# Hybrid trunk step on one core: the shift of the first modulation is carried through the input product as one more streamed column, and x is loaded by tiles

## What is computed

```python
def layer(x, c, pool_prefix, conv_prefix, pos0, norm1, ...):
    mod = jax.nn.silu(c) @ w_ada + b_ada
    sh1, sc1, g1, sh2, sc2, g2 = jnp.split(mod[:, None, :], 6, axis=-1)
    h = rmsnorm(x, norm1) * (1.0 + sc1) + sh1
    z = h @ w_in                       # 1024 x 2048
    u, gate_b, gate_c, val = jnp.split(z, ...)
    pool_out = pool_mixer(u, ...)      # trailing means, per-group map
    conv_out = gate_b * conv3(gate_c * val)
    x = x + g1 * (concat(pool_out, conv_out) @ w_out)
    h2 = rmsnorm(x, norm2) * (1.0 + sc2) + sh2
    x = x + g2 * moe(h2)               # top 4 of 32 experts
    return x, pool_state, conv_state
```

## Time and profile before

| | |
|---|---|
| median of 3 runs | 1287.76 us (1287.5, 1287.76, 1290.37) |
| span of the profiled execution | 1285.4 us |
| PE busy | 1250.7 us, 97% |
| input product starts | 37.93 us |
| feature 3 ends (fourth feature) | 67.51 us |
| feature 8 starts | 101.75 us |

### The profile page before, as it was taken

How to read it: one execution, slowest core, us unless ns; L and a number is a source line. 1 busy time by engine, 2 the same in 40 slices (tenths; PEclk the granted TensorE clock), 3 DMA queues, 4 the chain that set the end, 5 groups by cost and what they waited for, 6 DMA issues and landing times.

```text
span 1285.4 us, 32056 instructions
## 1 busy us (share of the span) xinstructions
PE 1250.7 (97%) x14081; PEld 639.7 (50%) x14081; DVE 522.6 (41%) x822; ACT 91.2 (7%) x170; POOL 248.7 (19%) x333
## 2 busy tenths in 40 slices
PE   4999999899999999999999999999999999999997
PEld 2787755534433444444444444444444444444454
DVE  1133314566333333333333334444444444443356
ACT  3210011210000000000000000000000000000002
POOL 4502300031222222111221111111111111122100
PEclk9999999899999999999999999999999999999998
DMA  9986861289999999999999999999999999999993
GB/s 349 265 334 231 303 255 81 105 366 428 421 425 425 425 426 426 420 424 421 425 423 421 422 425 424 425 427 425 419 423 427 426 423 424 428 427 423 423 424 154
DMA packets 62290, 487.45 MB, mean 379 GB/s; under 512 B 10387, under 2 KB 19203, under 8 KB 36913
## 3 DMA queue, kind: packets, MB, share of 16 engines
q1 hardware_dynamic: 47442, 455.92, 85.4%
q0 software_dynamic: 11632, 20.85, 4.6%
q10 hardware_dynamic: 3183, 10.21, 2.0%
HBM read 468.35 MB, written 25.88 MB: 384 GB/s over the span
## 4 chain that ended last, share of the span: by engine, by line
PE 95%; DVE 2%; ACT 1%; DMA 1%; issue 1%; SPq 0%; DVEq 0%; ACTq 0%
PE acc L2024 51%; PE acc L2049 24%; PE acc L964 9%; PE acc L1022 4%; PE acc L892 2%; PE acc L2133 1%; PE acc L2002 1%; DMA x_sb<-in_x_sample 1%; PE acc L910 1%; ACT junk L537 0%; PE acc L2149 0%; DVE picked L1684 0%; PE acc L994 0%; PE acc L1018 0%; PE acc L1034 0%
## 5 line engine op out<-in xcount | busy, mean ns | idle before, releaser
L2024 PE MATMUL acc<-raw,ht 128*32 128x512 f32 x2928 | 320.5, 592 | 0.0
L2024 PE MATMUL acc<-raw_b,ht 128*32 128x512 f32 x2928 | 320.5, 592 | 0.0
L1741 DVE TENSOR_TENSOR g_sb<-acc,bias_gu 128x768 f32<-128x768 f32 x32 | 30.6, 957 | 519.0 <-PE acc L2024 519.0
L1460 POOL DMA_INDIRECT rows<-h_rows,row_next x90 | 93.4, 1038 | 689.6 <-DVE row_next L1625 625.7
L2024 PEld LDWEIGHTS acc<-raw_b,ht 128*32 128x32 f32 x2928 | 111.0, 110 | 203.2 <-issue 203.2
L2024 PEld LDWEIGHTS acc<-raw,ht 128*32 128x32 f32 x2928 | 110.1, 110 | 190.6 <-issue 186.6
L2049 PE MATMUL acc<-raw_b,at 128*32 128x256 f32 x2976 | 166.9, 379 | 0.0
L2049 PE MATMUL acc<-raw,at 128*32 128x256 f32 x2976 | 166.9, 379 | 0.0
L2049 PEld LDWEIGHTS acc<-raw_b,at 128*32 128x32 f32 x2976 | 112.4, 110 | 61.4 <-issue 17.2
L2049 PEld LDWEIGHTS acc<-raw,at 128*32 128x32 f32 x2976 | 112.4, 110 | 48.2
L964 PE MATMUL acc<-h_t,raw 128*128 128x288 f32 (+1 forms) x512 | 118.8, 393 | 1.1 <-DVE h_t L732 1.1
(11 more groups left out here) (282 smaller groups left out, 677.1 us busy)
## 6 DMA issues: line engine op xcount, KB each, us to landing
raw<-in_w_down SPq DMA_DIRECT2D x33, 2048.0 KB, 15.7
raw<-in_w_gate SPq DMA_DIRECT2D x31, 2048.0 KB, 9.1
raw<-in_w_up SPq DMA_DIRECT2D x31, 2048.0 KB, 13.4
raw_b<-in_w_gate SPq DMA_DIRECT2D x31, 2048.0 KB, 10.1
raw_b<-in_w_up SPq DMA_DIRECT2D x31, 2048.0 KB
raw_b<-in_w_down SPq DMA_DIRECT2D x31, 2048.0 KB
raw<-in_w_ada SPq DMA_DIRECT2D x24, 1024.0 KB, 11.6
expert_rows<-zeros ACTq DMA_DIRECT2D x1, 8704.0 KB, 31.7
```

What stands on the lines that cost most here:

```text
L1460: pool.indirect_dma_start(rows[:, b, :], None, h2_quarter, bass.IndirectOffsetOnAxis(ap=idx[:, b:b + 1], axis=0), bounds_check=Q * NTOK - ...
L1741: dve.tensor_tensor(g_sb[:, :, :], gate_of(i, 0), plus(0), ALU.add).then_inc(g_read, 1)
L2024: mm = pe.matmul(gu_of(i)[b][q * TB:(q + 1) * TB, :].rearrange("p (m n) -> p m n", m=2), ht_of(i)[:, b, k, :], w[:, kk, :, q * CW:(q + 1) ...
```

## The change

The first modulation is split: only the scale is applied to `h_t` for the prompt. The shift vector is written as column 544 of `h_t` (`SHIFT_COL`), so that the second half of each feature streams 289 columns instead of 288, and the product of shift and w_in comes out beside the tokens. ACT copies that column to `z_shift` (`shift_of`), and everything that reads a feature of the prompt adds it: as the bias of the ACT copy, or as the scalar of a `scalar_tensor_tensor` on DVE. For the sample tokens scale and shift are still applied to `h_t` by DVE, the shift after the chunks of SH1. PE starts with the first halves of features 0, 1 and 2 as soon as the scale is in, then runs SH1, and half of feature 3's first half, the turning of the shift, the rest, and after that the four second halves. Features 2 and 3 need PSUM of their own for the first half (`z_early`) and are copied in two pieces. The order of chunks becomes SC1, in 0 and 1, SH1, in 2 and 3, G1, in 4 and 5, and from there on as before. x is loaded tile by tile and squared tile by tile, the tiles are turned into three PSUM tiles instead of one and earlier in the order, and the columns of scale and shift get PSUM and semaphores of their own. Two small memsets on POOL move ahead, so that ACT can start to square earlier. Some semaphores of the expert part are shared to make room (`tile_in`, `sum_step`); the waits there stay what they were.

```diff
@@
-        order = ada_chunks(SC1) + ada_chunks(SH1) + in_chunks(0, 4) + ada_chunks(G1) + in_chunks(4, 6)
+        order = ada_chunks(SC1) + in_chunks(0, 2) + ada_chunks(SH1) + in_chunks(2, 4) + ada_chunks(G1) + in_chunks(4, 6)
@@ sync
-            sp.dma_start(x_sb[:, 0:PT, :], x_prompt[0].rearrange("(t p) d -> p t d", p=P)).then_inc(x_loaded, 16)
-            sp.dma_start(x_sb[0:NS, PT, :], x_sample.rearrange("b t d -> (b t) d")).then_inc(x_loaded, 16)
+            for t in range(PT):
+                sp.dma_start(x_sb[:, t, :], x_prompt[0, t * P:(t + 1) * P, :]).then_inc(tile_in[t], 16)
+            sp.dma_start(x_sb[0:NS, PT, :], x_sample.rearrange("b t d -> (b t) d")).then_inc(tile_in[PT], 16)
@@ gpsimd
-            pool.wait_ge(h_mod_a, KT // 2)
+            pool.wait_ge(shift_col, 1)
@@ scalar
-            act.wait_ge(x_loaded, 32)
             act.wait_ge(consts, 2)
             for t in range(TT):
+                act.wait_ge(tile_in[t], 16)
                 square(t, 0)
...
+            for t in range(TT):
+                turned(f"n{t}", t, row_ps[t])
+            empty_cols(0)
...
             for k in range(KT // 2, KT):
                 act.activation(h_t[:, k, 0:SEQ], h_t[:, k, 0:SEQ], ACT.Identity,
-                               scale=cols[:, 0, k % 2, k // 2, 0:1],
-                               bias=cols[:, 1, k % 2, k // 2, 0:1]).then_inc(h_mod_a, 1)
+                               scale=cols[:, 0, k % 2, k // 2, 0:1]).then_inc(h_mod_a, 1)
+            empty_cols(1)
+            act.wait_ge(cols_free, 2)
+            act.activation(h_t[:, :, SHIFT_COL:SHIFT_COL + 1].rearrange("p (q h) o -> p h q o", h=KT // Q),
+                           cols[:, 1, :, :, 0:1], ACT.Copy).then_inc(shift_col, 1)
...
+            def shift_of(f):
+                act.wait_ge(z_done, f + 1)
+                act.activation(z_shift[:, f:f + 1], z_col[f % 2], ACT.Copy).then_inc(z_shift_ready, 1)
+
             def leave(f, dst, dst_s):
-                act.wait_ge(z_done, f + 1)
-                act.activation(dst.rearrange("p (b n) -> p b n", b=2), z_prompt[f % 2], ACT.Copy)\
-                    .then_inc(z_evac, 1)
+                shift_of(f)
+                act.wait_ge(z_shift_ready, f + 1)
+                halves = dst.rearrange("p (b n) -> p b n", b=2)
+                if f in z_early:
+                    for b in range(2):
+                        act.activation(halves[:, b, :], z_half(f, b)[:, 0:PH], ACT.Identity, bias=z_shift[:, f:f + 1])\
+                            .then_inc(z_evac, 1)
+                else:
+                    act.activation(halves, z_prompt[f % 2], ACT.Identity, bias=z_shift[:, f:f + 1]).then_inc(z_evac, 1)
                 act.activation(dst_s, z_sample[f % 2], ACT.Copy).then_inc(z_evac, 1)
@@ vector (features 8 to 11; 12 to 15 likewise)
-                dve.tensor_tensor(vext[...], z_prompt[f % 2], gate_c[...], ALU.mult)
+                dve.wait_ge(z_shift_ready, f + 1)
+                dve.scalar_tensor_tensor(out=vext[...], in0=z_prompt[f % 2], scalar=z_shift[:, f:f + 1],
+                                         in1=gate_c[...], op0=ALU.add, op1=ALU.mult)
@@ tensor
             ada_chunk(SC1, 0)
+            unit_transposes(0)
             ada_chunk(SC1, 1)
-            transposes("n0", 0, 0)
+            unit_transposes(1)
+            unit_transposes(2)
             ada_chunk(SC1, 2)
+            unit_transposes(3)
+            unit_transposes(4)
             ada_chunk(SC1, 3)
-            transposes("n1", 1, 0)
             pe.wait_ge(scale_ready, 1)
-            turn_cols("cols_sc", SC1)
...
+            turn_cols(SC1)
+            def half_product(f, b, k_first=0, k_end=KT):
+                w = chunk("in", f // 2)
+                lo_, hi_ = ((0, PH), (PH, SHIFT_COL + 1))[b]
+                for j in range(k_first, k_end):
+                    if f == 0 and b == 0:
+                        pe.wait_ge(*((h_mod_d, j + 1) if j < KT // 2 else (h_mod_a, j + 1 - KT // 2)))
+                    mm = pe.matmul(z_half(f, b), w[:, j, (f % 2) * P:(f % 2 + 1) * P], h_t[:, j, lo_:hi_],
+                                   start=(j == 0), stop=(j == KT - 1))
+                return mm
+            def early_chunks():
+                for f in range(3):
+                    half_product(f, 0)
+                ada(SH1)
+                half_product(3, 0, 0, KT // 2)
+                pe.wait_ge(ada_added, ADA_AT[SH1] + 1)
+                pe.wait_ge(cols_free, 1)
+                turn_cols(SH1)
+                half_product(3, 0, KT // 2, KT)
+                pe.wait_ge(h_mod_d, KT // 2 + KT // Q)
+                pe.wait_ge(shift_col, 1)
+                for f in range(4):
+                    if f >= 2:
+                        pe.wait_ge(z_evac, evacuated(f - 2))
+                    half_product(f, 1).then_inc(z_done, 1)
```

More of the change, by code:

```diff
@@ L128, in hybrid_step @@
         slot_loaded = [sem(f"slot_loaded{s}") for s in range(XSLOTS)]
+        tile_in = [sem(f"tile_in{t}") for t in range(TT)]
         part = ExitStack()
@@ L213, in hybrid_step, with z_half, evacuated @@
         z_sample = [z[:, 1, PH:PH + NS].rearrange("p (s t) -> p s t", t=DEC_T) for z in zt]
+        z_col = [z[:, 1, PH + NS:PH + NS + 1] for z in zt]
+        z_early = {2: acc_y[:, 1, 0:PH], 3: tp[:, 1, 0:PH]}
+        def z_half(f, b):
+            return z_early[f] if b == 0 and f in z_early else zt[f % 2][:, b, 0:PH if b == 0 else PH + NS + 1]
+        def evacuated(f):
+            return sum(3 if g in z_early else 2 for g in range(f + 1))
+        row_ps = [tp, acc_g, acc_u, tp, acc_g]
+        cols_ps = acc_y[:, 0, QW:2 * QW]
         pm_p = [tp[:, 0, :], tp[:, 1, :], acc_y[:, 1, :], tp[:, 0, :]]
@@ L607, in _ @@
                     empty_states()
+            for f in range(2 * GR, 4 * GR):
+                shift_of(f)
             for g in range(GR):
@@ L719, in unit_rows @@
                     .then_inc(h_ready, 1)
-            for t in range(3):
+            for t in range(TT):
                 unit_rows(t)
@@ L725, in _, with sample_half @@
             scale_rows(SC1, n1_rows)
[L726 to L730, removed]
+            dve.wait_ge(tp_free, TP["n4"] + 1)
+            dve.wait_ge(cols_free, 1)
             for k in range(KT // 2):
                 dve.tensor_scalar(h_t[:, k, 0:SEQ], h_t[:, k, 0:SEQ], cols[:, 0, k % 2, k // 2, 0:1],
[L733 to L739 removed]
+                                  None, ALU.mult).then_inc(h_mod_d, 1)
+            def sample_half(i, half):
+                v = h_t[:, :, SEQ:NTOK].rearrange("p (q h) (s t) -> p h q s t", q=Q, t=DEC_T)[:, half]
+                c = cols[:, i, half, :, 1:NC].unsqueeze(3).to_broadcast([P, Q, DEC_B, DEC_T])
+                return dve.tensor_tensor(v, v, c, (ALU.mult, ALU.add)[i])
+            for half in range(KT // Q):
+                step(sample_half(0, half))
+            add_ada(SH1)
+            dve.wait_ge(cols_free, 2)
+            for half in range(KT // Q):
+                sample_half(1, half).then_inc(h_mod_d, 1)
             def windows(src_, n, ext, buf):
@@ L810, in _ @@
                 v = conv[:, g, 0:SEQ].rearrange("p (b n) -> p b n", b=2)
-                dve.tensor_tensor(v, v, z_prompt[f % 2], ALU.mult).then_inc(conv_ready, 1)
+                dve.wait_ge(z_shift_ready, f + 1)
+                dve.scalar_tensor_tensor(out=v, in0=z_prompt[f % 2], scalar=z_shift[:, f:f + 1], in1=v,
+                                         op0=ALU.add, op1=ALU.mult).then_inc(conv_ready, 1)
                 v = by_seq(conv[:, g, SEQ:NTOK])
@@ L903, in take, with transposes @@
                     pe.wait_ge(tp_free, TP[name])
-            def transposes(name, t, base):
-                take(name)
+            def transposes(name, t, base, dst=tp, free=None):
+                if free is None:
+                    take(name)
+                else:
+                    pe.wait_ge(tp_free, free)
                 pe.wait_ge(h_ready, base + t + 1)
@@ L955, in project @@
                         pe.wait_ge(conv_s_ready, f - 3 * GR - 1)
[L956 to L969, removed]
+                    else:
+                        pe.wait_ge(z_evac, evacuated(f - 2))
+                    half_product(f, 0)
+                    half_product(f, 1).then_inc(z_done, 1)
+            early_chunks()
             pe.wait_ge(state_loaded, 16 * 4)
@@ L1212, in hybrid_step @@
             fn_loaded = sem("fn_loaded")
-            picked_in = [sem(f"picked_in{t}") for t in range(TT)]
             sum_step = sem("sum_step")
```

83 lines of the change are left out of this document (38 added, 45 removed).

## The result

The changed kernel takes 1292.1 us (median of 14 runs, 1290.03 to 1293.05) against 1288.29 us (1287.5 to 1290.37) for the kernel before: a ratio of 1.0026, with a 95% interval of 1.002 to 1.0033. It is slower by about 3.4 us. A second measurement gave 1.0031 (1.0021 to 1.0041). The prediction was 1290.0, with 1285 to 1298 and "same" as the likeliest. The loss is within the 0.3% that the prediction took as its line for "same", and yet clear of the noise.

A forecast was written before the change was run, and what follows sets the result against it. PE bounds the kernel (95% of the chain). Feature 3 -6.65 us, stand +6.2, clock +2.5, 289th column and small waits +0.2: +2.2 on 1285.4; the median stands 2.4 over that span: 1290.0 us, range 1285 to 1298.

The forecast's parts named there:

- "same": Whole kernel: time within 0.3% (3.9 us), with faster below 1283.9 and slower above 1291.6; chance 0.47.
- likeliest case: Whole kernel: early clock rise, PE stands before feature 8, clock falls; 1287.5 to 1292 us, chance 0.44.
- the early gain: Start through feature 3: product starts 10.5 us earlier, at 27.4; feature 3 ends 6.65 us earlier, at 60.85.
- the stand for chunk in 4: Before feature 8: PE waits 6.2 us, from 95.1 to 101.25, for that chunk to land.
- the half clock behind it: From feature 8: the pause lowers PE's clock, which returns after 3.4 to 5.6 us; price 2.5 us.
- rival 2: Start: tiles of x land together, squares start late, feature 3 ends some 4 us later; 1294 us, chance 0.08.
- The clock at the start: First chunks and tiles: unbroken work from 14.21, transposes included, raises PE's clock at 18.8, within 17.6 to 19.8.
- Rival 1: Start: transposes don't count, PE stays slow to the product at 32.5, nothing gained by feature 3; 1297.5 us, chance 0.26.
- The collision: Behind feature 3: five chunks (5.2 MB) start together with the zeros; chunk in 4 lands 40.4 us after feature 3 ends.
- rival 3: Behind feature 3: zeros start late or yield, chunks aren't held up, the gain stays whole; 1281.3 us, chance 0.12.
- Rival 4: Behind PE's wait before feature 8: the clock survives it; 1287.5 us, chance 0.06.
- The 289th column: Four second halves through feature 3: the extra column costs under 0.1 us; with small waits, 0.2 in the sum.

## Why the prediction was right

Its likeliest case happened: the early gain, the stand for chunk in 4 and the half clock behind it came in the order and nearly of the size that the working gave. In two profiles:

| step | forecast | changed kernel, 2 profiles |
|---|---|---|
| product starts | 27.4 | 29.33, 27.49 |
| feature 3 ends (Z) | 60.85 | 62.97, 61.12 |
| feature 8 starts | Z + 40.4 | Z + 41.2, Z + 41.3 |
| PE stands | 6.2 | 6.9, 7.0 |
| price of the clock | 2.5 | 2.6, 2.8 |

**The start.** The 27.49 of the second profile against 27.4 is in part luck. From the first matmul to the product the forecast had 13.2 us (27.4 - 14.21), and the profiles show 13.6 and 14.0; in the second the first chunk was 0.75 us early, which hid it. I had taken landing times of one execution as fixed; over the fourteen profiles of this study the first matmul on the chunk starts between 13.36 and 15.69, and in the first profile it was 1.5 us later than in the profile of before. Half of it or more is the clock, which rose 0.4 and 1.2 us later than taken (below). The first tile's row was ready at 16.8 in the first profile and 15.3 in the second, against 15.6 reckoned, and it was hidden behind the first chunk in both. In the first, ACT issued the loads of norm1 until 7.4 us, so that the first square started at 7.5 although its tile had landed at 4.7. The tiles landed one after another (the fourth square waited for its tile until 11.75), so rival 2 fell.

**The clock at the start.** It rose in the middle of chunks and tiles, 5.0 us after PE began in the first profile and 5.8 in the second, against the 4.6 that was taken. Rival 1 fell with that: here a stretch of transposes and chunks in turn raised the clock. The Trainium skill (TensorE: Matmul & The Clock Gate, PE-mode transpose) says that the full clock doesn't engage for transposes in TensorE's transpose mode. The profile lists these as matmuls and doesn't show the mode, and these rows don't show a stretch of transposes alone at the start, so they contradict only the rival that I built on it: with one tile of transposes between the first and the second chunk, the clock rose within or right behind the second.

**The collision.** This was the step that mattered, and it was right: the gain at feature 3 (6.65 forecast, 4.5 and 6.4 in the profiles) was given back, with interest, at feature 8. The equal counts of packets put feature 8 at Z + 40.4; it came 0.8 to 0.9 later. The rate was as taken (645 packets of in 4 in 8 us is 81 per us). What spoke for rival 3, that the zeros in the earlier trace rows began only when G1's fourth chunk was through, was not yielding: in the changed kernel they are issued at 63.22 and first move in the window 68 to 69, about 5 us later again, although G1's chunks are then still queued on q1. The experiments with late and with small zeros show the cause, each from its own side. In 2 and in 3 were in time, as reckoned (5.7 us and 6.0 us to landing).

**The clock behind the stand.** Predicted at 2.5. The kernel that kept PE busy shows 2.6 between profiles, and 1.5 to 2.3 in the time. Rival 4 fell.

**The size.** The forecast was +2.2 on the span. It came out at +5.4 between the two profiled executions: 1.9 more from the product's start (1.5 of it the late first chunk), 0.2 to feature 3, 0.8 from the distance to feature 8 and 0.15 from the clock. The second profile, with a span of 1289.0, gives +3.6. By the ratio it is +3.4. The term mis-sized in both profiles is the distance to feature 8, by 0.8 to 0.9. The median of 1292.1 is 2.1 over the forecast: above the 1287.5 to 1292 of the likeliest case by 0.1, and above the 1291.6 that was to be called slower. It counts as the same because the kernel before, measured beside it, was at 1288.29 and not at 1287.76, and the second ratio, 1.0031, is just past 0.3%: "same" had hardly any margin. The base was off too, the other way: in the other kernels the time of a profiled execution is 1.7 to 1.8 us over its span (1292.53 to 1290.8, 1281.21 to 1279.4), so the profiled execution of before ran in about 1287.2, and its median is 1.1 above. Longer half clocks in some executions are part of that: of the 74 executions of the kernel before that ran beside the experiments, 14 have a mean clock of 0.99 or less, with a median of 1290.2, and the other 60 a median of 1287.8. Rival 1's sum is off by 0.2: its terms give 1297.7, not 1297.5. The 289th column cost nothing that can be seen: 407 ns a record for 289 columns, against 406 for 288 in the kernel before.

## What to carry to other kernels

Moving a consumer earlier moves the releases of its buffers later or together: list which transfers each release starts, in the order of their queue, before counting the gain. A bulk transfer that nobody waits for isn't free beside loads that somebody does. Once both queues were moving data here, they moved equal counts of packets in every window shown, so the queue with the large packets won the bytes, and the cure was as small as another place or another packet size. Here, putting 8.7 MB of zeros late turned the change from 1.0026 into 0.9959. And the stand of 6.9 us cost 2.6 us more than its length, through the clock behind it; a sum from a profile should have a line for it. Last, a landing time read from one profile isn't fixed: the first chunk's moved by over 2 us between executions, as much as the whole forecast of +2.2.

## What was not expected of the hardware

- Short stands can cost the clock: with 2.6 us between SC1 and the product in which PE had 0.45 us of work, it fell in one profile (x in one DMA, 2.9 us lost) and not in seven others with the same stands. That idle matmuls there help isn't shown; in the stand of 6.9 us they kept the clock at full.
- The time at which the first megabyte chunk lands differs by over 2 us between executions, and not by the number of issues ahead of it: with four DMAs for x the first matmul started at 13.46 to 15.69, with one or two at 13.36 to 14.85.
